# Gate and up products of a feed-forward block: three column chunks in a row on the same weights

## The reference, cut to what matters

```
def rmsnorm(x, g):
    y = xf * lax.rsqrt(jnp.mean(xf * xf, axis=-1, keepdims=True) + NORM_EPS)
    return (y * g.astype(jnp.float32)).astype(x.dtype)

def swiglu(x, w_gate, w_up, w_down):
    return (jax.nn.silu(x @ w_gate) * (x @ w_up)) @ w_down

x = x + 0.5 * swiglu(rmsnorm(x, g_ffn1[l]), w1_gate[l], w1_up[l], w1_down[l])
...   # projection, sparse attention, state space branch, merge, output projection
x = x + 0.5 * swiglu(rmsnorm(x, g_ffn2[l]), w2_gate[l], w2_up[l], w2_down[l])
```

## Time and profile before

| | |
|---|---|
| time, median of 3 runs | 3165.23 us (3164.28 to 3169.18) |
| the profiled execution, span from the first to the last instruction | 3174.7 us |
| its mean granted TensorE clock | 0.902 of full |
| TensorE busy | 2761.3 us, 87% |
| VectorE busy | 1319.7 us, 42% |
| ScalarE busy | 688.8 us, 22% |
| GpSimd busy | 817.9 us, 26% |
| matmuls at L232 and L248 | 6336 and 3168 |

### The profile page before, as it was taken

One profiled execution on the slowest core, in us unless ns is written; L12 is line 12 of the kernel. 1 busy time (PEld: TensorE's weight loads), 2 busy tenths in 40 slices (PEclk: granted clock), 3 DMA queues, 4 the chain that ended last, 5 costly groups with the idle time before them and its releaser, 6 DMA issues.

```text
span 3174.7 us, 40963 instructions
## 1 busy us (share of the span) xinstructions
PE 2761.3 (87%) x16047; PEld 2514.3 (79%) x16047; DVE 1319.7 (42%) x2743; ACT 688.8 (22%) x1195; POOL 817.9 (26%) x521
## 2 busy tenths in 40 slices
PE   5999999999679999956689845688879999999996
PEld 4999999999658999944444544577869999999995
DVE  2223222222338999958731355133351222222224
ACT  4211111110133333313332410221041111111103
POOL 2522233232231112224300060022143232322210
PEclk8999999999889999976689555598989999999998
DMA  3211111110211322232222011142011111111101
GB/s 93 67 40 41 41 48 60 40 53 13 97 27 54 93 80 93 87 146 80 80 106 80 29 11 16 45 174 80 14 49 58 41 56 52 41 53 40 41 14 54
DMA packets 182798, 189.56 MB, mean 60 GB/s; under 512 B 18524, under 2 KB 164176, under 8 KB 179784
## 3 DMA queue, kind: packets, MB, share of 16 engines
q1 hardware_dynamic: 162632, 133.19, 14.0%
q0 software_dynamic: 2944, 35.65, 3.0%
q10 hardware_dynamic: 17072, 18.51, 1.6%
HBM read 160.10 MB, written 25.78 MB: 59 GB/s over the span
## 4 chain that ended last, share of the span: by engine, by line
PE 54%; DVE 11%; issue 3%; ACT 3%; DMA 1%; POOL 1%; SPq 0%; ACTq 0%; DVEq 0%; POOLq 0%
PE ps L232 15%; PE ps L574 12%; PE ps L248 8%; PE ps L1822 3%; PE ps L1808 3%; PE ps L1205 2%; PE ps L802 2%; DVE k_index_T_high L1122 1%; PE ps L824 1%; DVE new_small L1120 1%; PE ps L1522 1%; DVE probs L848 1%; PE ps L1562 1%; PE ps L1492 1%; PE ps L1520 1%
## 5 line engine op out<-in xcount | busy, mean ns | idle before, releaser
L232 PE MATMUL ps<-normed_split,f_weights_split 128*128 128x344 f32 x6336 | 1016.0, 323 | 26.0 <-issue 13.9
L232 PEld LDWEIGHTS ps<-normed_split,f_weights_split 128*128 128x128 f32 x6336 | 1011.0, 190 | 28.9 <-issue 15.3
L248 PE MATMUL ps<-f_hidden_split,f_down_split 128*128 128x344 f32 x3168 | 505.1, 321 | 11.9 <-issue 11.9
L248 PEld LDWEIGHTS ps<-f_hidden_split,f_down_split 128*128 128x128 f32 x3168 | 502.1, 189 | 12.4 <-issue 12.4
L279 DVE TENSOR_TENSOR f_hidden<-f_silu,ps 128x344 f32<-128x344 f32 x132 | 67.7, 513 | 877.3 <-PE ps L232 868.9
L574 PE MATMUL ps<-normed_split,in_weights_split 128*128 128x344 f32 (+1 forms) x2520 | 408.1, 323 | 14.8 <-POOL normed_split L110 13.6
L574 PEld LDWEIGHTS ps<-normed_split,in_weights_split 128*128 128x128 f32 (+1 forms) x2520 | 399.9, 188 | 19.3 <-POOL normed_split L110 14.3
L289 DVE SCALAR_TENSOR_TENSOR x_T<-ps,x_T 128x344 f32<-128x344 f32 x528 | 272.9, 517 | 232.5 <-PE ps L248 232.4
L196 POOL TENSOR_TENSOR f_hidden_split<-f_hidden,f_hidden_split 128x344 fp32r<-128x344 f32 x132 | 122.7, 930 | 595.4 <-DVE f_hidden_split L282 595.4
L188 POOL TENSOR_TENSOR f_weights_split<-f_weights_raw,f_weights_split 128x1024 fp32r<-128x1024 f32 x88 | 210.3, 2410 | 81.9 <-ACT f_weights_split L150 81.9
L202 POOL TENSOR_TENSOR f_down_split<-f_down_raw,f_down_split 128x1024 fp32r<-128x1024 f32 x44 | 104.2, 2388 | 436.2 <-ACT f_down_split L166 436.2
(11 more groups left out here) (303 smaller groups left out, 2624.7 us busy)
## 6 DMA issues: line engine op xcount, KB each, us to landing
f_weights_raw<-in_w_gate SPq DMA_DIRECT2D x44, 512.0 KB, 3.9
f_weights_raw<-in_w_up SPq DMA_DIRECT2D x44, 512.0 KB, 4.2
f_down_raw<-in_w_down SPq DMA_DIRECT2D x44, 512.0 KB, 3.5
in_weights_raw<-in_w_in SPq DMA_DIRECT2D x34, 512.0 KB, 3.8
gates_T<-projected ACTq DMA_DIRECT2D x16, 516.0 KB, 2.6
gates<-gates_T SPq DMA_DIRECT2D x16, 516.0 KB, 4.5
x_meanwhile<-x_T SPq DMA_DIRECT2D x1, 4128.0 KB, 15.1
x_T<-x_meanwhile SPq DMA_DIRECT2D x1, 4128.0 KB, 17.7
```

The source lines that it names most:

```text
L232: mm = nc.tensor.matmul(m.ps[:, NCH * half + c, :CH], m.wh[:, 2 * e + half, a, k * P:(k + 1) * P], m.xn[:, k, b, cols(c)], start=(k == 0 a ...
L248: mm = nc.tensor.matmul(m.ps[:, 6 + n % 2, :CH], m.dh[:, e, a, o * P:(o + 1) * P], m.hh[:, 2 * par + e, b, cols(c)], start=(e == 0 and t = ...
```

## The change

Inside `gate_up`, half (gate, then up) becomes the outermost loop, then the slice k of the contraction, then the pass, and the chunk c becomes the innermost. Three matmuls in a row now have the same weights and write to three different banks; high weights serve six in a row. The waits for `s.silu` and `s.mul` stand before the first matmul of each chunk, the counts of `s.gate` and `s.up` on the last of each chunk. For the first slice there is one wait for `s.lo` of all three chunks. Nothing else is edited; the instructions of the other engines are the same in the same order.

```
 def ffn_pe(nc, pe, m, s):
     def gate_up(f, e, used=True):
         pe.wait_ge(s.wlo, s.was.wlo + 2 * f + 2)
-        for c in range(NCH):
-            if not used:
-                pe.wait_ge(s.lo, s.was.lo + KD * (c + 1))
-            for half, done in ((0, s.gate), (1, s.up)):
-                if used:
-                    pe.wait_ge((s.silu, s.mul)[half], s.was.silu + NCH * (f - 1) + c + 1)
-                for k in range(KD):
-                    for n, (a, b) in enumerate(PASSES):
+        if not used:
+            pe.wait_ge(s.lo, s.was.lo + KD * NCH)
+        for half, done in ((0, s.gate), (1, s.up)):
+            for k in range(KD):
+                for n, (a, b) in enumerate(PASSES):
+                    for c in range(NCH):
+                        if used and k == 0 and n == 0:
+                            pe.wait_ge((s.silu, s.mul)[half], s.was.silu + NCH * (f - 1) + c + 1)
                         mm = nc.tensor.matmul(m.ps[:, NCH * half + c, :CH],
                                               m.wh[:, 2 * e + half, a, k * P:(k + 1) * P],
                                               m.xn[:, k, b, cols(c)],
                                               start=(k == 0 and n == 0), stop=(k == KD - 1 and n == 2))
-                mm.then_inc(done, 1)
+                        if k == KD - 1 and n == 2:
+                            mm.then_inc(done, 1)
```

## The result

The changed kernel takes 3233.81 us (median of 4 runs, 3233.2 to 3244.89), the kernel before 3165.27 us on the same chip (median of 4, 3164.28 to 3169.18): a ratio of 1.0235, 95% interval 1.0203 to 1.0268. It is slower by 68.5 us (the two medians alone give 1.0217). The forecast was 3240 (3208 to 3265).

The account below looks back on a forecast made before the run. TensorE, busy 87% of the span, was taken to bound the kernel; the profiled 3174.7 us plus 35.0 for block starts and 40.0 for downs gave 3249.7, less 9.5 to the median: 3240 us, range 3208 to 3265.

Parts of the forecast that it names:

- The pace: Matmuls of L232: repeated weights and bank changes alter nothing, 157.6 ns each stays, 0 us.
- The low bound: L232: part of a possible 25 us gain from bank changes, 4 ns each, kept for the range's low end.
- the turnaround of a load that the rival guessed at: L232: 14.3 ns of each 157.6 ns perhaps turnaround of weights or sums, removable by reuse; full reuse chance 0.04.
- the reuse rival: L232: repeated weights pay, in full 91 us (3149 us, chance 0.04) or in part 40 us (3200 us, 0.03).
- The start of a block: First slice of each block: all 144 matmuls wait for the norm's last low part; 17.5 us lost, two blocks 35.0.
- The start of down(p): down(0) to down(9): TensorE waits for VectorE's first addition behind three chunks; 2.00 us each, 20 make 40.0 us.
- The sum: Whole kernel: 3174.7 + 35.0 + 40.0 = 3249.7 us of span, median 9.5 us below, so 3240 us.
- a gap at a loop round: Heads of loop rounds: TensorE's unexplained 3.04 us gaps may come or go, a few being 8 us either way.
- The things put at nothing: Gate and up halves: waits for silu and L279, GpSimd's weight split and register work stay hidden, 0 us.
- The covered waits: Downs: VectorE gets its first addition in time, only the block start is lost; 3200 us, chance 0.04.
- The fall of the clock: Start of each down: 1.9 us idle lowers the clock, 20 x 1.75 = 35 us, 3275 us; chance 0.07.
- The rival in which cycling through banks lets the clock fall: gate_ups: one clock fall in each of 44, 77 us, 3317 us; chance 0.02 for banks and clock.

Follow-up runs that it names:

- second profile of the kernel before: The kernel before, with nothing changed, profiled once more: 3167.92 us.
- additions first alone: Changed kernel, VectorE's three products and casts of the odd slice put singly behind the first six additions of the following down: 3195.08 us.
- with the first slice put back: Changed kernel with that same VectorE order, and each block's first slice again chunk by chunk: 3158.81 us, ratio 0.9943 to the kernel before.

## Why the prediction was right

**The pace.** Zero was taken, 157.6 ns. Measured 157.1, a gain of 3.4 us over 6336 matmuls. The low bound had kept room for a part of 25. The two rows that the choice rested on were the right ones: the loads are still 6336, and repeated weights had the same distance. What sets the distance is not the turnaround of a load that the rival guessed at, since the pace went with the columns (117.8 ns at 256). Neither form of the reuse rival came; the pace would have had to fall to 145.8 ns.

**The start of a block.** The forecast was 17.5 us each: 15.1 for 96 matmuls and 2.4 for the start at half clock. In the chain, TensorE's piece is 93.00 us and two matmuls (0.31) now and was 75.91, 17.4 more, of which the pace gives back 0.3: 17.7. The first stretch after the 22.9 us of idle time ran at half clock, the next at full:

```profile
2399.90:2405.60 5.70, 5.63 (x20) 5.66 (x21) 0.00 (x0) 1.99 (x2) 4.57 (x2) 0.50 0.33 95
2405.70:2425.20 19.50, 19.50 (x126) 19.50 (x125) 0.00 (x0) 1.16 (x3) 0.00 (x0) 1.00 0.09 26
```

**The start of down(p).** The forecast was 2.00 us each. The pair grew by 69.77 - 68.02 = 1.75, with 0.16 given back by the pace: 1.91. Each link came as worked out: first product two matmuls early, casts held to 0.75 where 0.64 was expected, the first addition lengthened by nothing, TensorE 0.05 us behind its end. From the first product to the end of the first addition the sum had 3.79 us; measured are 2496.77 - 2493.05 = 3.72. Three differences nearly cancel: a held cast 0.1 longer; the distance from the first product to the second 0.80 where 0.89 was taken; and the first addition, which starts 0.07 before the last cast's end (2496.27 against 2496.34) where it was taken to start behind it. That the total came so close is in part luck. With 20 of them the term is 38.2 us, not 40.0.

**The sum.** 35.4 + 38.2 - 3.4 = 70 us against 75 forecast and 68.5 between the medians. Between the two profiled spans it is 57.4, since the first profile of the kernel before was 9.4 us above its median and the one of the changed kernel 1.7 below; the number to trust was the one made against the median. One thing the sum didn't move is a gap at a loop round, which the forecast said may come or go. The changed kernel has four,

```profile
PE ps L232 <- issue: 10.3, 4, 2.8
```

and the kernel before five, 13.9 us of idle time; the one less is worth 2.5 us and 1.8 of slower matmuls (2.45 + 47.20 - 45.40 = 4.25 above). That makes 66 us of the 70. The span of the second profile of the kernel before is 3166.1 us, 66.0 below that of the changed kernel; that they meet so closely is luck, since the gaps' lengths vary too. The things put at nothing came so: TensorE's list of waits has none at L232 for a silu or a product.

**The rivals.** The covered waits (3200 us) fell with the twenty waits in the list. The fall of the clock did not happen at 1.65 us and did in 16 of 20 cases at 2.85. The rival in which cycling through banks lets the clock fall did not come: with another bank at every matmul the clock is 1.00 over the 19.5 us shown above, and the pace 157.1.

## What to carry to other kernels

Before a loop order is changed for the sake of the weights, ask what sets the distance of two matmuls; where it goes with the columns, as here, repeated weights are worth next to nothing. What such an order does change is when results become ready: they now come all at once and at the end, so look at who consumes them singly, what stands behind that in the consumer's order, and which first wait used to be met piece by piece. The cure for the second loss was in the consumer: the products and casts that nobody waits for yet were moved behind the first additions, and TensorE no longer waits in any down. The first loss needs the old order in the first slice.

## What the runs showed of the hardware

- A matmul of fp32r columns takes about 0.45 ns per column and 2 to 3 ns beside it at the full clock (157.6 ns for 344, 117.8 for 256), and whether its weights are new or repeated and whether the bank changes makes 0.5 ns at most. Two points make this line. 344 columns at one per cycle of 2.4 GHz would be 143.
- A cast from SBUF to SBUF on VectorE that comes under a subtraction on GpSimd waits for its end: 0.75 us in place of 0.34. Additions that read PSUM are not held: the two from 2496.27 take 0.93 us together with a subtraction under way from 2496.42.
- Idle time and the granted clock: 1.65 us never lowered it (20 of 20 downs of the changed kernel), and the 2.15 us ahead of the third chunk neither. Between 2.4 and 3.1 us it went either way, and the length alone didn't decide: at the loop rounds the 2.45 us above were followed by 1.8 us more for 288 matmuls, the 2.50 us ahead of the last round of the changed kernel by 0.26 more for 286 (45.20 against 44.94), with the clock at 1.00:

```profile
3015.00 2.50 issue
3017.51 45.20 PE ps L232 x286
```

- The index scores, code that no experiment touched, ran in 27.3 us or in 38.2 us. The first 23 us of it in two profiles, additions first alone and with the first slice put back (columns as above):

```profile
952.00:975.00 23.00, 20.98 (x48) 11.71 (x48) 9.86 (x14) 8.49 (x15) 0.00 (x0) 0.53 0.00 1
```

```profile
931.50:954.50 23.00, 20.22 (x70) 10.24 (x71) 15.33 (x20) 12.99 (x20) 0.00 (x0) 1.00 0.01 1
```

48 records of TensorE at a clock of 0.53, or 70 at 1.00. TensorE and ScalarE alternate there, and the slower TensorE runs the longer each turn. It is 11 us between profiles that no edit of the blocks explains.
